# Decode rows' mLSTM projections: full-precision products on four column groups of one PSUM bank instead of split products

## The reference

```
h = rmsnorm(x, g_mix)
q_m, k_m, v_m, o_m, i_pre, f_pre, q_a, k_a, v_a = split_cols(h @ w_in)   # q_m, k_m, v_m, o_m: 512 columns each
h_til, c1, n1, m1 = mlstm_chunkwise(q_m, k_m * 128**-0.5, v_m, gates, c0, n0, m0)   # 4 heads of 128
h_m = sigmoid(o_m) * rmsnorm(h_til, g_head)
```

## Time and profile before

| | |
|---|---|
| median of 3 runs | 2598.69 us |
| the profiled execution, its own time | 2596.14 us |
| its span | 2594.5 us |
| mean granted TensorE clock | 0.997 |
| TensorE matmul busy | 2555.3 us |
| VectorE busy | 1885.6 us |
| ScalarE busy | 903.9 us |

### The profile page before, as it was taken

One profiled execution on the slowest core, in us unless ns is written; L12 is line 12 of the kernel. 1 busy time (PEld: TensorE's weight loads), 2 busy tenths in 40 slices (PEclk: granted clock), 3 DMA queues, 4 the chain that ended last, 5 costly groups with the idle time before them and its releaser, 6 DMA issues.

```text
span 2594.5 us, 40780 instructions
## 1 busy us (share of the span) xinstructions
PE 2555.3 (98%) x14143; PEld 2222.8 (86%) x14143; DVE 1885.6 (73%) x3281; ACT 903.9 (35%) x2097; POOL 79.3 (3%) x170
## 2 busy tenths in 40 slices
PE   8999999999999999999999999999999999999999
PEld 6888888878888869999999999999888888888887
DVE  7777777775555578777777788888888877885443
ACT  5333333454444443222222333232332332343322
POOL 0000000000000010000000000000000000000010
PEclk9999999999999999999999999999999999999999
DMA  5112111452232346222222532323342222233223
GB/s 211 57 57 84 57 57 52 173 161 98 104 111 97 112 151 214 65 65 65 65 65 65 202 131 66 96 66 96 127 151 81 65 81 66 79 142 136 86 73 108
DMA packets 163367, 261.86 MB, mean 101 GB/s; under 512 B 11440, under 2 KB 111256, under 8 KB 162520
## 3 DMA queue, kind: packets, MB, share of 16 engines
q1 hardware_dynamic: 160936, 252.29, 29.0%
q0 software_dynamic: 2352, 8.52, 1.0%
HBM read 199.99 MB, written 60.62 MB: 100 GB/s over the span
## 4 chain that ended last, share of the span: by engine, by line
PE 90%; DVE 5%; issue 2%; ACT 1%; DMA 1%; POOL 0%; ACTq 0%; DVEq 0%; SPq 0%; POOLq 0%
PE m_proj L112 13%; PE m_proj L114 12%; PE m_proj L113 12%; PE m_turned L112 6%; PE m_turned L114 6%; PE m_turned L113 6%; PE m_acc L112 5%; PE m_acc L114 5%; PE m_acc L113 5%; PE m_pair L112 4%; PE m_pair L113 4%; PE m_pair L114 4%; PE m_pair L1274 1%; PE m_turned L1282 1%; PE m_acc L1299 1%
## 5 line engine op out<-in xcount | busy, mean ns | idle before, releaser
L2115 ACT ACTIVATE f_up_hi<-f_sums 128x512 fp32r<-128x512 f32 x138 | 85.8, 622 | 512.2 <-DVE f_sums L2410 487.1
L2441 DVE TENSOR_TENSOR f_part<-f_part,m_acc 128x384 f32<-128x384 f32 (+2 forms) x240 | 119.3, 514 | 139.8 <-PE m_acc L114 137.0
L112 PE MATMUL m_proj<-f_down_hi,f_uT_hi 128*128 128x512 f32 x476 | 188.8, 397 | 2.5 <-DVE f_acc L2484 2.5
L114 PE MATMUL m_proj<-f_down_hi,f_uT_lo 128*128 128x512 f32 x476 | 185.5, 390 | 0.0
L113 PE MATMUL m_proj<-f_down_lo,f_uT_hi 128*128 128x512 f32 x476 | 185.4, 390 | 0.0
L112 PE MATMUL m_turned<-f_down_hi,f_uT_hi 128*128 128x512 f32 x472 | 183.9, 390 | 1.0 <-DVE f_acc L2476 0.9
L113 PE MATMUL m_turned<-f_down_lo,f_uT_hi 128*128 128x512 f32 x472 | 184.1, 390 | 0.0
L114 PE MATMUL m_turned<-f_down_hi,f_uT_lo 128*128 128x512 f32 x472 | 183.9, 390 | 0.0
L2484 DVE TENSOR_TENSOR f_acc<-f_acc,m_proj 128x1024 f32<-128x1024 f32 x118 | 143.9, 1220 | 45.3 <-PE m_proj L114 45.1
L2484 DVE TENSOR_TENSOR f_acc<-f_acc,m_turned 128x1024 f32<-128x1024 f32 x131 | 151.7, 1158 | 27.4 <-PE m_turned L114 25.5
L2139 ACT ACTIVATE f_uT_hi<-f_part 128x256 fp32r<-128x256 f32 (+2 forms) x300 | 92.2, 364 | 202.2 <-PE m_turned L114 122.4
(11 more groups left out here) (452 smaller groups left out, 7321.0 us busy)
## 6 DMA issues: line engine op xcount, KB each, us to landing
f_down_raw<-in_w_down SPq DMA_DIRECT2D x96, 512.0 KB, 5.2
f_up_raw<-in_w_up SPq DMA_DIRECT2D x92, 512.0 KB, 5.3
hT_hi_kept<-m_hT_hi SPq DMA_DIRECT2D x17, 512.0 KB, 5.0
hT_lo_kept<-m_hT_lo SPq DMA_DIRECT2D x17, 512.0 KB, 5.7
a_hT_hi<-hT_hi_kept SPq DMA_DIRECT2D x17, 512.0 KB, 3.7
a_hT_lo<-hT_lo_kept SPq DMA_DIRECT2D x17, 512.0 KB, 4.6
m_x<-in_x_prompt SPq DMA_DIRECT2D x16, 512.0 KB, 4.3
a_x_sum<-in_x_prompt SPq DMA_DIRECT2D x16, 512.0 KB, 6.3
```

Source lines behind the costliest of these rows:

```text
L112: eng.matmul(out, lh(k), rh(k), start=f, stop=False)
L114: ins = eng.matmul(out, ll(k), rh(k), start=False, stop=e)
L2115: act.activation(up_hi[:, q], weight(q), ACT.Copy).then_inc(up_hi_made, 1)
L2441: dve.tensor_tensor(part[out][:, 0:w], part[other][:, 0:w], up_ps[bank][:, 0:w], ALU.add).then_inc(combined, 1)
```

## The change

In round 16 the split products for q, k, v and the first half of o are replaced by `project_dec`. It uses `h_dec`, a float32 copy of the turned decode activations (32 columns for each chunk), made by one more ScalarE copy in `split_h`, in the unused slot of `x`. For each of the 8 chunks, for the high and then the low part of the weights (read as float32), it issues four matmuls, which write the four row quarters of the one bank `proj[0]`: q, k, v (512 columns each) and o (256). It runs in three pieces: chunks 0 to 4 where q and k stood, chunks 5 and 6 where v stood, chunk 7 where o stood. All four semaphores q_ps, k_ps, v_ps, o_ps get their count for the decode rows from the last four matmuls of chunk 7. ScalarE takes q and k after the o exponential; VectorE takes v after C_new; both from their row quarter. TensorE's wait for o_sb moves from before attention's project_kv(tile 0) to before its project_q(tile 0). SyncE's program and the waits of ScalarE's wq_hi are not touched.

```diff
+    DEC_CHUNKS = [range(0, 5), range(5, 7), range(7, KC)]
+    h_dec = x[:, 1 - NT % 2, 0:KC * DEC].rearrange("p (c n) -> p c n", c=KC)
...
+            if t.n < P:
+                act.activation(h_dec, turned[:, :, 0:DEC], ACT.Copy)
             act.activation(hT_hi[:, t.slot, :, 0:t.n], turned[:, :, 0:t.n], ACT.Copy).then_inc(h_hi, 1)
...
-                if not first_round(r):
+                if not first_round(r) and not on_round(r, NT):
                     take_q(cur)
-            if exists(i) and not first_round(r):
+            if exists(i) and not first_round(r) and not on_round(r, NT):
                 take_k(cur)
...
-                act.activation(o[0:n, slot, 0:MW // 2], proj[1][0:n, 0:MW // 2], ACT.Exp, scale=-1.0).then_inc(o_sb, 1)
+                o_from = proj[0][row_quarter(3)] if on_round(r, NT) else proj[1][0:n]
+                act.activation(o[0:n, slot, 0:MW // 2], o_from[:, 0:MW // 2], ACT.Exp, scale=-1.0).then_inc(o_sb, 1)
+                if on_round(r, NT):
+                    take_q(cur)
+                    take_k(cur)
...
+        def project_dec(chunks):
+            for c in chunks:
+                for part in (0, 1):
+                    for j, (weights, done) in enumerate(((w_q, q_ps), (w_k, k_ps), (w_v, v_ps), (w_o, o_ps))):
+                        w = weights(c)[part].bitcast(F32)
+                        ins = pe.matmul(proj[0][row_quarter(j), 0:MW // 2 if j == 3 else MW], h_dec[:, c, :], w,
+                                        start=c == 0 and part == 0, stop=c == KC - 1 and part == 1)
+                        if c == KC - 1 and part == 1:
+                            ins.then_inc(done, 1)
...
-                    project(proj[0], cur, w_q, q_ps)
+                    if on_round(r, NT):
+                        project_dec(DEC_CHUNKS[0])
+                    else:
+                        project(proj[0], cur, w_q, q_ps)
...
-            if exists(i) and not first_round(r):
+            if exists(i) and not first_round(r) and not on_round(r, NT):
                 all_of(pe, o_sb, i - 1)
                 project(proj[1], cur, w_k, k_ps)
...
-                    all_of(pe, q_sb, i)
-                    project(proj[0], cur, w_v, v_ps)
+                    if on_round(r, NT):
+                        project_dec(DEC_CHUNKS[1])
+                    else:
+                        all_of(pe, q_sb, i)
+                        project(proj[0], cur, w_v, v_ps)
...
-                if not first_round(r):
+                if on_round(r, NT):
+                    project_dec(DEC_CHUNKS[2])
+                elif not first_round(r):
                     all_of(pe, k_sb, i)
                     project(proj[1][:, 0:MW // 2], cur, w_o, o_ps)
...
-                all_of(dve, v_ps, i)
-                dve.tensor_copy(v[0:n, slot, :, 0:QK], proj[0][0:n, :].rearrange("p (h d) -> p h d", h=HEADS)).then_inc(v_sb, 1)
+                if not on_round(r, NT):
+                    all_of(dve, v_ps, i)
+                    dve.tensor_copy(v[0:n, slot, :, 0:QK], proj[0][0:n, :].rearrange("p (h d) -> p h d", h=HEADS)).then_inc(v_sb, 1)
...
                 ins.then_inc(C_made, 1)
+                if on_round(r, NT):
+                    all_of(dve, v_ps, i)
+                    dve.tensor_copy(v[0:n, slot, :, 0:QK], proj[0][row_quarter(2), :].rearrange("p (h d) -> p h d", h=HEADS)).then_inc(v_sb, 1)
...
         pe.wait_ge(*m.v_sb)
+        pe.wait_ge(*m.o_sb)
         project_q(t, range(KC)).then_inc(q_ps, 1)
         yield
-        pe.wait_ge(*m.o_sb)
         project_kv(t)
```

More of the change, by code:

```diff
@@ L517, in take_k @@
             all_of(act, k_ps, t.i)
-            src = first_k if first_round(t.i) else proj[1]
-            act.activation(k[0:t.n, t.slot, :], src[0:t.n, :], ACT.Copy, scale=QK ** -0.5).then_inc(k_sb, 1)
+            src = first_k[0:P] if first_round(t.i) else proj[1][0:P] if t.n == P else proj[0][row_quarter(1)]
+            act.activation(k[0:t.n, t.slot, :], src, ACT.Copy, scale=QK ** -0.5).then_inc(k_sb, 1)
         def body(r, slot):
```

## The result

The changed kernel takes 2610.86 us (median of 6 runs, 2609.14 to 2612.52) against 2598.73 us before: +12.1 us, a ratio of 1.0049 with a 95% interval of 1.0040 to 1.0059. Forecast was 2609.5 us. Its profiled execution took 2612.52 us, the longest of the six, with a span of 2610.9 us.

A forecast was written before the change was run, and what follows sets the result against it. The prediction took TensorE, busy 98% of the span, as the bound. A stall of 8.7 us, with the 5.0 saved inside it, plus 2.5 for the clock gave +11.2 us on 2598.69: 2609.9, stated as 2609.5, range 2604 to 2614 us.

The forecast's parts named there:

- wq_raw issued: SyncE's queue: q_ps gets its count with chunk 7, so the load is issued at 495.5 us, before at 481.70.
- halves land, after the issue: Two 1 MB halves of wq_raw, with the stores done: 4.9 and 7.3 us after issue, before 6.3 and 8.5.
- its shift, less 0.7: TensorE's round 17 start: L644 at 510.1 in place of 501.46 us, 8.7 us later, bounds 7.0 to 11.4.
- TensorE saves 5.0 us: Round 16's projections on TensorE: 14.5 us in place of 19.5, bounds 3.5 to 5.9, the saving spent waiting.
- The load of wq_raw is the cost: Attention's weight load, issued 13.8 us after q's old end, delays ScalarE, VectorE and TensorE; shift 8.7 us.
- The decode rows' gate steps are held behind it: ScalarE's queue: gate rows, o exponential and q and k copies stand behind wq_hi; L559 at 509.5, not 500.81 us.
- part 3: Landing of wq_raw: halves at 500.4 and 502.9 us; hT of tile 0 behind them shifts alike, wanted much later.
- The clock: TensorE after 10.6 us idle: half rate for 5.2 us from 510.1, costing 2.5 us in project_q, bounds 0 to 4.
- The crossings: TensorE going into and out of three packed blocks: 0.2 us each, 0.6 in all; 0.13 read from the trace.
- the drain of a whole recorded latency: TensorE: about 0.4 us lost at each of six crossings would make the projections 16.3 us, the sum 1.8 higher.
- The rival on the faster side: Round 16: loads have unseen slack, so TensorE's saving counts and it ends 5.0 us early, 2593.7 us; chance 0.06.
- the groups of four do run side by side: Packed products on TensorE: 0.434 us a group of four; the rival, not side by side, +34.7, 2644 us, chance 0.04.

The follow-up runs named there:

- e4: Kernel before, with halves of q and k packed first in one bank, then v and o's first half in the other, 256 columns wide: 2598.06 us, ratio 0.9997.
- e7: e4 with one useless float32 matmul of 512 columns ahead of L734 and one behind it, filling TensorE's two gaps: 2595.01 us, ratio 0.9990.
- e2: Kernel before, unpacked, with SyncE's wait for q_ps ahead of the wq_raw load made a wait for o_ps: 2613.99 us, ratio 1.0062.
- e1: Changed kernel with all 16 sets of the packed projection in one block, where chunks 0 to 4 stood: 2604.91 us, ratio 1.0025.
- e3: Changed kernel with ScalarE's wq_hi put behind its whole round 16 and VectorE's first four wq_lo behind L895: 2605.78 us, ratio 1.0027.
- e5: Changed kernel with 14 useless float32 matmuls in TensorE's idle stretch, 11 ahead of L728 and 3 behind it: 2607.60 us, ratio 1.0037.
- e6: e4 with chunks 6 and 7 of v and o moved to where o stood, and the v copy behind C_new: 2597.80 us, ratio 0.9999.

## Why the prediction was right

The median came out 1.4 us above the forecast. The steps compare like this (the changed kernel's trace is 0.7 us late before the changed round, see above, so 0.7 is to be added to each predicted time):

| step | predicted, us | measured, us |
|---|---|---|
| a group of four, 512 wide | 0.434 | 0.43 |
| the first block ends, L665 of round 16 | 485.0 | 485.59 |
| wq_raw issued | 495.5 | 496.14 |
| halves land, after the issue | 4.9 and 7.3 | 5.0 and 7.2 |
| C_new made | 505.8 | 506.58 |
| L567 (was L559) starts | 509.5 | 510.48 |
| L883 (was L853) starts | 509.8 | 510.82 |
| round 17's L665 (was L644) | 510.1 | 511.14 |
| its shift, less 0.7 | 8.7 | 9.0 |
| the clock's part, at the copy of k | 2.5 | 2.5 |

- *TensorE saves 5.0 us, all of it spent waiting.* Both show in the trace; e4 and e7 show what it is worth where q and k are finished first: nothing by e4's median, 2.9 us with the gaps filled.
- *The load of wq_raw is the cost.* e2 makes the same loss without the change (+15.8, expected +14.8 on the same arithmetic), e1 takes 5.4 us of it back for a load 5.4 us earlier. Two single edits, one on either kernel, agree.
- *The decode rows' gate steps are held behind it by the order of the queues.* Right as a mechanism, and e3 puts it at 4.5 us of 12.1, some of that clock. But my part 3 said of hT of tile 0 that it was "wanted much later". That is true only while the queues hold TensorE up: in e3, hT was the next thing late, by 7.05 us. As a statement on slack it was wrong, and e3's expectation, which rested on it, missed by 4.8 us.
- *The clock.* Half rate from 499.8 to 516.8 us, 5.7 us of it after round 17 began, where I took 5.2 from the earlier trace rows. e5 gives 2.4 us between medians. I had taken 3.67 us of idleness as the nearest row for a fall of the clock; e4 shows that two gaps of 1.31 and 0.80 us within 3 us can be followed by one, and e5 that two of 1.12 and 0.72 us need not be. That the half rate would be there behind 10.6 us of idleness was right. That it cost 2.5 us was in part luck: the 5.2 us came from a single row, and the stay, 17 us in all here, was 3.4 us in e6 and 6.8 in e4.
- *The crossings.* About 0.1 us each, as the forecast had them; the drain of a whole recorded latency that I weighed beside the Trainium skill's rule (TensorEngine Tiling, "Key Properties") does not show. The first block's last group starts at 485.06 and takes 0.43, to 485.49, and L665 starts at 485.59.
- *The rival on the faster side* (slack in the loads) is excluded by e2, and the groups of four do run side by side. What stays open: why the lag in the profiled execution grows from 12.2 us at 526 to 16.4 at the end. Matched instruction by instruction, one microsecond arises before 550 us, two around 1000 us, where the granted clock is lower, and one around 1505 us, at a clock of 1.00 in both kernels; there TensorE waits twice for VectorE's low parts of the MLP weights (L2447, 0.41 and 0.42 us), before only once. Why was not followed up.

## What to carry to other kernels

Several results packed side by side into one product are all finished together, at the end. Before packing, look at who waits for each of them, and first at a DMA queue that reuses the operands' memory: here the first result released 2 MB of loads, and finishing it 14 us later cost 12 us, while a packing in the order of need (e4: q and k before v and o, in other widths) cost nothing. An engine's queue is in order, so a late load is paid by everything written behind its first user. And when one wait is shortened on a TensorE-bound kernel, check the granted clock behind the new gaps, in more than one execution if you can: here two matmuls of no use in gaps of about a microsecond were worth 2.8 us, while other gaps of that size cost no clock at all.

## What the runs showed of the hardware

- Four float32 matmuls of 128x32 by 128x512, on four column groups of one bank, advance 0.43 us a group of records (two groups a call), the narrower o (256 columns) beside them not slowing them; three groups of 256 columns advance 0.21 us (e4, 485.73 to 485.94). Going into or out of this form costs about 0.1 us.
- The granted clock fell to 0.5 after idle gaps of 1.31 and 0.80 us close together (e4), and was back at 1.00 after 6.8 us; with the gaps filled by one float32 matmul each, it stayed at 1.00 (e7). After one and the same gap of 1.65 us it stayed at 1.00 in the kernel before and fell in the changed one. The page "TensorE: Matmul & The Clock Gate" of the Trainium skill, in "Why this matters for your kernels", tells one to avoid idle gaps between bursts of matmuls; e4 and e7 agree.
- 1 MB halves of wq_raw landed 5.0 and 7.2 us after issue with the stores 14 us past, against 6.3 and 8.5 behind 1 MB of stores.
